# Four RMS norms and a last one: squares summed in column strips, roots spread by picked rows, two units that end one after the other

## The chip, the cores and the metric

The kernel runs on one core of a Trainium2 chip. The metric is device time in microseconds (us), and lower is better. TensorE (PE) multiplies and writes to PSUM; VectorE (DVE) and ScalarE (ACT) do the work by element; GpSimd (POOL) here only splits weights; SyncE (SP) issues most DMAs. The engines run their own instruction streams in order and wait for one another through semaphores.

## What is computed

One inference step of a small decoder of two layers, for a prompt of 1024 tokens and for 8 requests of 8 tokens. Layer 0 mixes with a gated linear recurrence, layer 1 with forgetting attention; each is followed by a gated feed-forward part (FFN) with a short convolution. The change concerns only the norms ahead of the projections:

```python
def _rmsnorm(x, g):
    n = x32 * lax.rsqrt(jnp.mean(x32 * x32, axis=-1, keepdims=True) + EPS)
    return n * g
def _modnorm(x, g, shift, scale):
    return _rmsnorm(x, g) * (1.0 + scale[:, None, :]) + shift[:, None, :]
...
    hn = _modnorm(x, norm_mix_g[l], sh1, sc1)      # before the mixer
    hn = _modnorm(x, norm_ffn_g[l], sh2, sc2)      # before the FFN
    hk = _modnorm(x, kv_norm_g, kv_shift, kv_scale)  # before K, V and forget logits
y = _rmsnorm(x, final_norm_g)
```

## The kernel before

**Layout.** The residual stream X holds channels on partitions: 8 tiles (k = 0 to 7) of 128 channels, each with T = 1090 columns (1026 for the prompt with its padding, 64 for the samples). A norm sums over channels, so over partitions and over the 8 tiles. A projection multiplies in three passes at the precision of fp32: the normed tile is kept as a high part HH and a low part HL, a unit of weights (8 k-tiles of 128 x 128) as WH and WL, and PE forms WH·HH, WL·HH and WH·HL, each in three pieces of 342, 342 and 406 columns.

**Norms.** There are six uses: norm 0 (recurrence), 1 (FFN of layer 0), 2 (K and V), 3 (queries; same X as norm 2, so its roots are reused), 4 (FFN of layer 1) and the final one, which goes straight to the output. ACT squares each tile into SQ (L1037), DVE adds seven of them into ACC (L1384). PE sums over partitions (L673 for ACC, L677 for the last SQ): the data are the weights, in nine blocks of 128 columns, and a column of ones streams, so that the sums land as 128 x 9. DVE and ACT form the reciprocal root on S9 (L1394, L1042, L1397 to L1400: mean, square root, reciprocal, one Newton step). DVE multiplies the identity by the nine columns (DIAG, L1402), PE spreads them over all partitions (L685), ACT copies them into RS (L1046).

**First use.** DVE scales a tile into TN (`scaled`, L1410), ACT adds the shift and rounds it into HH (`high`, L1053), DVE takes the rest as HL (`lowered`, L1427). The 64 sample columns of all 8 tiles go together (L1415 to L1419 on DVE, L1056 on ACT, L1426 on DVE), between tiles 0 and 1, and ACT signals the first HH tile only after them. PE takes the tiles as they come in `two_units` (L652): for each k both units u = 0 and 1, the three passes in turn, so that the two units end together.

**Order around it.** After `two_units` each later unit of the stage is one `unit_job` (L627). Its weights must be split by POOL (WH at L564, WL at L567), and POOL may overwrite a slot of WH and WL only when ACT has seen that the unit before in this slot is done (`got`, L1028). DMAs keep the raw weights ahead. ACT must also have emptied the slot in PSUM (`free`).

## Time and profile before

| | us |
|---|---|
| device time, median of 3 runs | 3282.46 (3279.54 to 3283.14) |
| profiled execution, device time | 3284.32 |
| its span, first to last instruction | 3282.9 |
| PE busy | 3060.2 (93% of the span) |
| POOL, DVE, ACT busy | 1121.4, 1372.9, 879.4 |
| granted PE clock, mean | 0.967 of full speed |

The profiled execution is 1.86 us above the median, and 1.4 us of it lie outside the span. In the rows below a timeline gives the start, the length, the engine, line and operation of each merged group, the number of records, and in brackets how long the engine had been idle and what ended that. A matmul of plain fp32 data leaves two records. The clock is a share of 2.4 GHz.

### The profile page before, as it was taken

The numbers are of one execution on the slowest core, as the hardware profiler recorded it, in microseconds if no ns is written. First come the engines' busy times: TensorE is split into PE (matmuls) and PEld (weight loads), VectorE is DVE, ScalarE is ACT, GpSimd is POOL, SyncE is SP. The second block draws the span as 40 slices with busy tenths as digits, with TensorE's granted clock in tenths as the row PEclk, the third lists the DMA queues.
The fourth block names the chain that finished last, engine by engine and source line by source line (L and its number), as shares of the span: only waits on it lengthen the run. The fifth ranks groups of instructions, "written<-read, shape, count | busy, mean of one in ns | idle before, by whom it ended". The sixth has DMA issues, their size and how long they took to land.

```text
span 3282.9 us, 49150 instructions
## 1 busy us (share of the span) xinstructions
PE 3060.2 (93%) x19242; PEld 2877.5 (88%) x19242; DVE 1372.9 (42%) x2024; ACT 879.4 (27%) x1453; POOL 1121.4 (34%) x571
## 2 busy tenths in 40 slices
PE   6999979899999999997997988888899999999996
PEld 4878859799999999997997866657899999999996
DVE  5345382443434444345103165542443434344344
ACT  3143170241312112122212145541141213121121
POOL 1312305333333333332332255524333333333331
PEclk9999989899999999998998989999899999999997
DMA  6644612111111111110543554664111111111111
GB/s 220 215 150 151 226 68 79 38 51 42 41 45 45 45 44 39 45 45 28 168 144 142 151 128 106 175 268 166 38 39 45 45 45 41 42 45 45 45 44 61
DMA packets 99465, 295.58 MB, mean 90 GB/s; under 512 B 14001, under 2 KB 15409, under 8 KB 99105
## 3 DMA queue, kind: packets, MB, share of 16 engines
q1 hardware_dynamic: 85616, 244.52, 22.5%
q10 hardware_dynamic: 13744, 49.61, 4.4%
q8 instruction: 73, 1.20, 0.1%
q14 instruction: 32, 0.25, 0.0%
HBM read 253.98 MB, written 40.10 MB: 90 GB/s over the span
## 4 chain that ended last, share of the span: by engine, by line
PE 65%; issue 11%; DVE 4%; POOL 3%; ACT 2%; DMA 1%; ACTq 0%; SPq 0%; POOLq 0%; DVEq 0%
PE PS L627 56%; PE PS L895 2%; POOL WH L564 2%; PE PS L878 2%; POOL WL L567 1%; PE PS L862 1%; PE PS L863 1%; ACT PX L1282 1%; PE PS L652 1%; DMA KB<-in_cache_k 0%; DMA X<-in_xT 0%; PE PS L909 0%; ACT PT L1272 0%; DVE X L1863 0%; PE PS L941 0%
## 5 line engine op out<-in xcount | busy, mean ns | idle before, releaser
L564 POOL TENSOR_TENSOR WH<-WRAW,ZERO 128x1024 fp32r<-128x1024 f32 x214 | 410.7, 1919 | 1868.9 <-ACTq L1028 1289.9
L627 PE MATMUL PS<-HH,WH 128*128 128x342 f32 (+1 forms) x3144 | 702.0, 332 | 28.1 <-POOL WL L567 24.9
L627 PE MATMUL PS<-HL,WH 128*128 128x342 f32 (+1 forms) x3144 | 701.9, 332 | 0.0
L627 PE MATMUL PS<-HH,WL 128*128 128x342 f32 (+1 forms) x3144 | 699.4, 331 | 0.0
L627 PEld LDWEIGHTS PS<-HH,WH 128*128 128x128 f32 x3144 | 559.3, 190 | 36.6 <-issue 18.8
L627 PEld LDWEIGHTS PS<-HH,WL 128*128 128x128 f32 x3144 | 562.3, 190 | 1.7
L627 PEld LDWEIGHTS PS<-HL,WH 128*128 128x128 f32 x3144 | 563.1, 190 | 0.2
L567 POOL TENSOR_TENSOR WL<-WRAW,WH 128x1024 fp32r<-128x1024 f32 x214 | 544.8, 2546 | 16.8
L1638 DVE SCALAR_TENSOR_TENSOR FC<-FU,FCW,FC 128x1026 f32<-128x1026 f32 x96 | 239.7, 2497 | 587.6 <-ACT FC L1140 587.6
L627 PE MATMUL PS<-AH,WH 128*128 128x342 f32 (+1 forms) x1152 | 256.9, 331 | 6.4 <-DVE AL L1656 4.9
L627 PE MATMUL PS<-AH,WL 128*128 128x342 f32 (+1 forms) x1152 | 255.4, 330 | 0.0
L627 PE MATMUL PS<-AL,WH 128*128 128x342 f32 (+1 forms) x1152 | 255.0, 330 | 0.0
L1135 ACT ACTIVATE FU<-PS 128x1026 f32<-128x1026 f32 x96 | 98.9, 1030 | 566.8 <-PE PS L627 566.8
L1448 DVE TENSOR_TENSOR XS<-PS,MOD 128x64 f32<-128x64 f32 x112 | 25.1, 224 | 499.2 <-PE PS L627 496.3
L1144 ACT ACTIVATE AH<-FC 128x1090 f32 (+1 forms) x48 | 53.7, 1120 | 660.2 <-DVE FC L1654 660.2
L627 PEld LDWEIGHTS PS<-AH,WH 128*128 128x128 f32 x1152 | 205.0, 190 | 8.5 <-DVE AL L1656 5.6
L627 PEld LDWEIGHTS PS<-AH,WL 128*128 128x128 f32 x1152 | 205.3, 189 | 0.9
L627 PEld LDWEIGHTS PS<-AL,WH 128*128 128x128 f32 x1152 | 205.2, 189 | 0.3
L1450 DVE SCALAR_TENSOR_TENSOR X<-PS,MOD,X 128x1026 f32 (+1 forms) x112 | 143.9, 1284 | 0.0
L1646 DVE SCALAR_TENSOR_TENSOR FC<-FU,FCW,FC 128x1026 f32<-128x1026 f32 x96 | 127.7, 1330 | 0.0
L1037 ACT ACTIVATE SQ<-X 128x1090 f32 x40 | 44.5, 1116 | 300.1 <-DVE X L1453 288.1
L1139 ACT ACTIVATE FC<-PS,FCW 128x1026 f32<-128x1026 f32 x96 | 116.5, 1214 | 0.0
(273 smaller groups left out, 3575.3 us busy)
## 6 DMA issues: line engine op xcount, KB each, us to landing
WRAW<-in_wstream SPq DMA_DIRECT2D x214, 512.0 KB, 3.5
MS<-in_mod_w SPq DMA_DIRECT2D x96, 512.0 KB, 6.8
KB<-in_cache_k SPq DMA_DIRECT2D x32, 512.0 KB, 8.8
VB<-in_cache_v SPq DMA_DIRECT2D x32, 512.0 KB, 8.0
K<-k_split SPq DMA_DIRECT2D x48, 256.0 KB
Q<-q_split SPq DMA_DIRECT2D x48, 256.0 KB
out_kv<-STG ACTq DMA_DIRECT2D x16, 545.0 KB, 3.2
MU<-in_mod_w SPq DMA_DIRECT2D x16, 512.0 KB, 12.5
```

The costliest lines, as they stand in the source:

```text
L564: pool.tensor_tensor(WH[:, u, :], WRAW[:, u, :], ZERO[:].broadcast_to([P, UNIT]), ALU.add).then_inc(hi.sem, 1)
L567: pool.tensor_tensor(WL[:, u, :], WRAW[:, u, :], WH[:, u, :].bitcast(F32), ALU.subtract).then_inc(S["split_done"], 1)
L627: mm = pe.matmul(PS[:, o:o + hi - lo], lhs(n), rhs[:, k, lo:hi], start=first and n == 0 and m == 0, stop=last and n == len(kts) - 1 and m ...
L878: mm = pe.transpose(PS[:, o + n * P:o + (n + 1) * P], tile[:, w_ + kt * P:w_ + (kt + 1) * P], ID[:])
L895: mm = pe.matmul(PS[rows, o + c:o + end], VS[p % 2][:, kt, rows], PT[:, e, st % RING, c:end], start=(i == 0 and c == lo), stop=True, skip_ ...
L1037: act.activation(SQ[:, u, :], X[:, i * 2 + u, :], ACT.Square).then_inc(S["act_sq"], 1)
L1135: act.activation(three(FU[:, s, 2:2 + S0]), prompt(s), ACT.Copy)
L1139: act.activation(three(FC[:, s, 0:S0]), prompt(s), ACT.Identity, **par)
L1144: act.activation(AH[:, c, :], FC[:, 0, :], ACT.Copy).then_inc(S["f_hi"], 1)
L1450: STT(three(X[:, k, 0:S0]), prompt(s), MOD[:, gate + k, 0:1], three(X[:, k, 0:S0]), ALU.mult, ALU.add).then_inc(free[s], 1)
L1638: STT(FC[:, s, 0:S0], FU[:, s, 1:1 + S0], FCW[:, idx, 1:2], FC[:, s, 0:S0], ALU.mult, ALU.add)\
L1646: STT(FC[:, s, 0:S0], FU[:, s, 0:S0], FCW[:, idx, 0:1], FC[:, s, 0:S0], ALU.mult, ALU.add)
```

## The change

Five things are changed. **Sums:** the ones become the weights, 32 columns of them, and the squares stream in four pieces of 273 columns, each into its own strip of 32 partitions; the sums land on 128 partitions x 273 columns, 32 rows alike in each strip. **Roots:** the steps on DVE and ACT work on 128 x 273 (SV). A square root of a single element (WARM) stands ahead of the wait for the mean. DIAG is gone: PE multiplies SV by a column of the identity repeated 128 times, which picks row 32j, so that quarter j appears on all partitions. **First tile:** ACT copies, DVE scales and ACT rounds tile 0 quarter by quarter, and PE starts unit 0 on the first two column pieces. **Samples:** they come after tile 1. **Two units:** the lows of tiles 0 and 1 come after the highs of both, and tiles 5, 6, 7 are done for unit 0 first, then for unit 1. Norm 3 has only the last two. The core of the diff (memory and semaphore names left out):

```diff
@@ -100,17 +100,19 @@
     return done // KT - 1 if done // KT > (done - bursts(unit)) // KT else None
-SPREAD = ((0, 3), (3, 6), (6, 9))
-def position(j):
-    return min(P * j, T - P)
+QUARTER = 273
+ROOT_AT = (0, 1536, 2048, 2560)
+def quarter(j):
+    return min(QUARTER * j, T - QUARTER)
 U_RG, U_OUT, U_FFN, U_LF, U_D = 2 * RT, 2 * KT, 2 * FT + NG * GC, 2, KT
 UNITS_1 = U_RG + U_OUT + U_FFN + U_LF + 3 * U_D
 UNITS_2 = U_D + U_FFN
+SHARED = 5
 PIECES = ((0, PC), (PC, 2 * PC), (2 * PC, T))
...
@@ -635,24 +638,50 @@
             pe.wait_ge(free[u].sem, free[u].next())
             job(u, tiles(WH, u), tiles(WL, u), xh, xl, range(KT), fresh=fresh).then_inc(ready[u], 1)
-        def two_units():
+        def two_units(roots_in_psum=True):
+            def part_of(k, u, pieces, lows):
+                for m, (w_, x) in enumerate(((WH, HL),) if lows else ((WH, HH), (WL, HH))):
+                    for c in pieces:
+                        lo, hi = PIECES[c]
+                        o = SLOT[u] + 512 * c
+                        mm = pe.matmul(PS[:, o:o + hi - lo], w_[:, u, k * P:(k + 1) * P], x[:, k, lo:hi],
+                                       start=k == 0 and m == 0 and not lows, stop=k == KT - 1 and lows)
+                return mm
             for u in range(2):
                 pe.wait_ge(split.sem, split.next())
+            if roots_in_psum:
+                for c in range(2):
+                    pe.wait_ge(part.sem, part.next())
+                    part_of(0, 0, (c,), False)
+            for u in range(2):
                 pe.wait_ge(free[u].sem, free[u].next())
-            for k in range(KT):
-                for m, (w_, x) in enumerate(((WH, HH), (WL, HH), (WH, HL))):
-                    if m == 0:
-                        pe.wait_ge(hh.sem, hh.next())
-                    if m == 2:
-                        pe.wait_ge(hn.sem, hn.next())
-                    for u in range(2):
-                        for c, (lo, hi) in enumerate(PIECES):
-                            o = SLOT[u] + 512 * c
-                            mm = pe.matmul(PS[:, o:o + hi - lo], w_[:, u, k * P:(k + 1) * P], x[:, k, lo:hi],
-                                           start=k == 0 and m == 0, stop=k == KT - 1 and m == 2)
-                        if k == KT - 1 and m == 2:
-                            mm.then_inc(ready[u], 1)
+            pe.wait_ge(hh.sem, hh.next())
+            for u in range(roots_in_psum, 2):
+                part_of(0, u, (0, 1), False)
+            pe.wait_ge(hh.sem, hh.next())
+            for u in range(2):
+                part_of(1, u, (0, 1), False)
+            pe.wait_ge(his.sem, his.next())
+            for k in range(2):
+                for u in range(2):
+                    part_of(k, u, (2,), False)
+            for k in range(2):
+                pe.wait_ge(hn.sem, hn.next())
+                for u in range(2):
+                    part_of(k, u, (0, 1, 2), True)
+            for k, units in [(k, (0, 1)) for k in range(2, SHARED)] + [(k, (u,)) for u in range(2) for k in range(SHARED, KT)]:
+                if units[0] == 0:
+                    pe.wait_ge(hh.sem, hh.next())
+                for u in units:
+                    part_of(k, u, (0, 1, 2), False)
+                if units[0] == 0:
+                    pe.wait_ge(hn.sem, hn.next())
+                for u in units:
+                    mm = part_of(k, u, (0, 1, 2), True)
+                    if k == KT - 1:
+                        mm.then_inc(ready[u], 1)
         def proj(xh, xl, pairs, fresh=None):
...
@@ -669,23 +698,18 @@
             pe.wait_ge(acc.sem, acc.next(KT - 1))
             acc.next()
             pe.wait_ge(free[0].sem, free[0].next())
-            for j in range(9):
-                pe.matmul(PS[:, 1524 + j:1525 + j], ACC[:, position(j):position(j) + P], ONES[:, 0:1],
-                          start=j == 0, stop=True, skip_group_check=True)
+            for j in range(4):
+                pe.matmul(PS[32 * j:32 * j + 32, 0:QUARTER], ONES[:, 0:32], ACC[:, quarter(j):quarter(j) + QUARTER],
+                          start=True, stop=True, skip_group_check=True)
             pe.wait_ge(sq.sem, sq.next(KT))
-            for j in range(9):
-                mm = pe.matmul(PS[:, 1524 + j:1525 + j], SQ[:, 1, position(j):position(j) + P], ONES[:, 0:1],
+            for j in range(4):
+                mm = pe.matmul(PS[32 * j:32 * j + 32, 0:QUARTER], ONES[:, 0:32], SQ[:, 1, quarter(j):quarter(j) + QUARTER],
                                start=False, stop=True, skip_group_check=True)
             mm.then_inc(ready[0], 1)
-            for c, (a, b) in enumerate(SPREAD):
-                pe.wait_ge(diag.sem, diag.next())
-                for lo, hi in ((a, min(b, 8)), (8, b)):
-                    if hi > lo:
-                        n = min(P * hi, T) - P * lo
-                        mm = pe.matmul(PS[:, 512 * c + P * (lo - a):512 * c + P * (lo - a) + n], ONES[:],
-                                       DIAG[:].rearrange("p j x -> p (j x)")[:, P * hi - n:P * hi], start=lo == a, stop=True,
-                                       skip_group_check=True)
-                mm.then_inc(S["rs_psum"], 1)
+            pe.wait_ge(rows_done.sem, rows_done.next())
+            for j, o in enumerate(ROOT_AT):
+                pe.matmul(PS[:, o:o + QUARTER], ID[:, 32 * j:32 * j + 1].broadcast_to([P, P]), SV[:, 2, :],
+                          start=True, stop=True).then_inc(S["rs_psum"], 1)
         def mod_product(x, buf, sem, landed):
...
@@ -1038,23 +1062,37 @@
         def roots():
             ready[0].next()
+            act.activation(WARM[:], ZERO[:], ACT.Sqrt)
             act.wait_ge(var.sem, var.next())
-            act.activation(S9[:, 1, :], S9[:, 0, :], ACT.Sqrt).then_inc(S["rs_root"], 1)
-            for c, (a, b) in enumerate(SPREAD):
-                act.wait_ge(spread.sem, spread.next())
-                n = min(P * b, T) - P * a
-                ins = act.activation(RS[:, P * a:P * a + n], PS[:, 512 * c:512 * c + n], ACT.Copy)
+            act.activation(SV[:, 1, :], SV[:, 0, :], ACT.Sqrt).then_inc(S["rs_root"], 1)
+        def kept(j):
+            act.wait_ge(spread.sem, spread.next())
+            a, b = QUARTER * j, min(QUARTER * j + QUARTER, T)
+            o = ROOT_AT[j] + a - quarter(j)
+            ins = act.activation(RS[:, a:b], PS[:, o:o + b - a], ACT.Copy)
             ins.then_inc(S["act_root"], 1)
         def high(n):
             for k in range(KT):
-                act.wait_ge(tn.sem, tn.next())
                 sh = NORMS[n][0] + k
-                ins = act.activation(HH[:, k, 0:S0], TN[:, k % 2, 0:S0], ACT.Identity, bias=MOD[:, sh, 0:1])
-                if k == 0:
+                if k == 0 and n != 3:
+                    kept(0)
+                    for j in range(4):
+                        if j < 3:
+                            kept(j + 1)
+                        act.wait_ge(tn.sem, tn.next())
+                        a, b = QUARTER * j, min(QUARTER * j + QUARTER, S0)
+                        ins = act.activation(HH[:, 0, a:b], TN[:, 0, a:b], ACT.Identity, bias=MOD[:, sh, 0:1])
+                        if j in (1, 2):
+                            ins.then_inc(S["hi_part"], 1)
+                else:
+                    act.wait_ge(tn.sem, tn.next())
+                    ins = act.activation(HH[:, k, 0:S0], TN[:, k % 2, 0:S0], ACT.Identity, bias=MOD[:, sh, 0:1])
+                ins.then_inc(S["act_hi"], 1)
+                if k == 1:
                     act.wait_ge(S["dve_tns"], n + 1)
-                    ins = act.activation(HH[:, :, S0:T], TNS[:], ACT.Copy)
-                ins.then_inc(S["act_hi"], 1)
+                    act.activation(HH[:, :, S0:T], TNS[:], ACT.Copy).then_inc(S["act_his"], 1)
         def norm(n, sums=True):
             if sums:
...
@@ -1390,18 +1430,22 @@
             sq.next()
             dve.sem_inc(accs.sem, 1)
             accs.next()
-            v, r, y, z = (S9[:, n, :] for n in range(4))
-            TSC(v, PS[:, 1524:1533], 1.0 / D, EPS, ALU.mult, ALU.add).then_inc(S["dve_var"], 1)
+            v, r, y, z = (SV[:, n, :] for n in range(4))
+            TSC(v, PS[:, 0:QUARTER], 1.0 / D, EPS, ALU.mult, ALU.add).then_inc(S["dve_var"], 1)
             dve.wait_ge(var.sem, var.next())
             dve.wait_ge(roots.sem, roots.next())
             chain(dve.reciprocal(y, r))
             chain(STT(z, y, -0.5, y, ALU.mult, ALU.mult))
             chain(TT(z, z, v, ALU.mult))
-            chain(STT(y, z, 1.5, y, ALU.add, ALU.mult))
-            for a, b in SPREAD:
-                TT(DIAG[:, a:b, :], ID[:].unsqueeze(1).broadcast_to([P, b - a, P]),
-                   y[:, a:b].unsqueeze(2).broadcast_to([P, b - a, P]), ALU.mult).then_inc(S["rs_diag"], 1)
-            dve.wait_ge(root.sem, root.next())
+            STT(y, z, 1.5, y, ALU.add, ALU.mult).then_inc(S["rs_rows"], 1)
+        def first_scaled(n):
+            for j in range(4):
+                a, b = QUARTER * j, min(QUARTER * j + QUARTER, S0)
+                dve.wait_ge(root.sem, root.next())
+                STT(TN[:, 0, a:b], X[:, 0, a:b], MOD[:, NORMS[n][1], 0:1], RS[:, a:b], ALU.mult, ALU.mult)\
+                    .then_inc(S["dve_tn"], 1)
             dve.sem_inc(free[0], 1)
         def scaled(n, k):
...
@@ -1422,18 +1466,22 @@
             dve.wait_ge(hi.sem, hi.next())
             sh = NORMS[n][0] + k
+            ins = STT(HL[:, k, 0:S0], TN[:, k % 2, 0:S0], MOD[:, sh, 0:1], HH[:, k, 0:S0].bitcast(F32), ALU.add, ALU.subtract)
             if k == 0:
-                TT(HL[:, :, S0:T], TNS[:], HH[:, :, S0:T].bitcast(F32), ALU.subtract)
-            STT(HL[:, k, 0:S0], TN[:, k % 2, 0:S0], MOD[:, sh, 0:1], HH[:, k, 0:S0].bitcast(F32), ALU.add, ALU.subtract)\
-                .then_inc(los.sem, 1)
+                dve.wait_ge(S["act_his"], n + 1)
+                ins = TT(HL[:, :, S0:T], TNS[:], HH[:, :, S0:T].bitcast(F32), ALU.subtract)
+            ins.then_inc(los.sem, 1)
             los.next()
         def norm(n, sums=True):
             if sums:
                 rms()
-            scaled(n, 0)
+            if n != 3:
+                first_scaled(n)
+            else:
+                scaled(n, 0)
+            scaled(n, 1)
             scaled_samples(n)
-            scaled(n, 1)
             for k in range(KT):
                 lowered(n, k)
                 if k + 2 < KT:
...
@@ -1859,6 +1907,8 @@
         dve.wait_ge(xdone.sem, xdone.next(KT))
         ffn(1)
         rms()
+        dve.wait_ge(root.sem, root.next(4))
+        dve.sem_inc(free[0], 1)
         for k in range(KT):
             STT(X[:, k, :], X[:, k, :], NGAIN[:, 5, k:k + 1], RS[:], ALU.mult, ALU.mult).then_inc(S["dve_tn"], 1)
```

On PE, from the sums of norm 1 into its two units (PS is PSUM, ID the identity; the operand that streams is named first). Before:

```order
L673 MATMUL PS<-ONES,ACC 128x1 x9
L677 MATMUL PS<-ONES,SQ 128x1 x9
L685 MATMUL PS<-DIAG,ONES 128x384 x2
L685 MATMUL PS<-DIAG,ONES 128x256
L685 MATMUL PS<-DIAG,ONES 128x66
L652 MATMUL PS<-HH,WH 128x342 x2
L652 MATMUL PS<-HH,WH 128x406
L652 MATMUL PS<-HH,WH 128x342 x2
L652 MATMUL PS<-HH,WH 128x406
```

After:

```order
L702 MATMUL PS<-ACC,ONES 32x273 x4
L706 MATMUL PS<-SQ,ONES 32x273 x4
L711 MATMUL PS<-SV,ID 128x273 x4
L648 MATMUL PS<-HH,WH 128x342
L648 MATMUL PS<-HH,WL 128x342
L648 MATMUL PS<-HH,WH 128x342
L648 MATMUL PS<-HH,WL 128x342
L648 MATMUL PS<-HH,WH 128x342 x2
L648 MATMUL PS<-HH,WL 128x342 x2
L648 MATMUL PS<-HH,WH 128x342 x2
```

Eighteen sums with data as weights became eight with ones as weights, and the first two pieces of tile 0 of unit 0 stand alone ahead of the rest.

On PE, the end of the same two units and the first job of the next pair. Before:

```order
L652 MATMUL PS<-HH,WL 128x342 x2
L652 MATMUL PS<-HH,WL 128x406
L652 MATMUL PS<-HH,WL 128x342 x2
L652 MATMUL PS<-HH,WL 128x406
L652 MATMUL PS<-HL,WH 128x342 x2
L652 MATMUL PS<-HL,WH 128x406
L652 MATMUL PS<-HL,WH 128x342 x2
L652 MATMUL PS<-HL,WH 128x406
L135 UNCONDITIONAL_BRANCH
L135 ISA
L635 REGISTER_ALU
L627 MATMUL PS<-HH,WH 128x342 x2
```

After:

```order
L648 MATMUL PS<-HL,WH 128x342 x2
L648 MATMUL PS<-HL,WH 128x406
L648 MATMUL PS<-HH,WH 128x342 x2
L648 MATMUL PS<-HH,WH 128x406
L648 MATMUL PS<-HH,WL 128x342 x2
L648 MATMUL PS<-HH,WL 128x406
L648 MATMUL PS<-HL,WH 128x342 x2
L648 MATMUL PS<-HL,WH 128x406
L137 UNCONDITIONAL_BRANCH
L137 ISA
L638 REGISTER_ALU
L630 MATMUL PS<-HH,WH 128x342 x2
```

Before, unit 0 ends two rows ahead of unit 1 (the last four HL rows are 0, 0, 1, 1); after, these rows are all of unit 1, and unit 0 has ended eighteen rows ahead of the end.

On ACT, norm 2, behind the store of the FFN's state. Before:

```order
L1164 DMA out_fst<-FST 128x864
L1042 ACT_TABLE_LOAD [waits dve_var]
L1042 ACTIVATE S_92<-S_92 128x9 [waits ffn_out]
L1046 ACTIVATE RS<-PS 128x384 [waits rs_psum] x2
L1046 ACTIVATE RS<-PS 128x322 [waits rs_psum]
L1053 ACTIVATE HH<-TN,MOD 128x1026 [waits dve_tn]
```

After:

```order
L1202 DMA out_fst<-FST 128x864
L1065 ACT_TABLE_LOAD
L1065 ACTIVATE WARM<-ZERO 128x1 [waits ffn_out]
L1067 ACTIVATE SV<-SV 128x273 [waits dve_var]
L1073 ACTIVATE RS<-PS 128x273 [waits rs_psum] x2
L1086 ACTIVATE HH<-TN,MOD 128x273 [waits dve_tn]
L1073 ACTIVATE RS<-PS 128x273 [waits rs_psum]
L1086 ACTIVATE HH<-TN,MOD 128x273 [waits dve_tn]
L1073 ACTIVATE RS<-PS 128x271 [waits rs_psum]
```

The load of the table for the square root carried the wait for the mean; now it carries none, and the copies of the roots alternate with the quarters of tile 0.

## Rows read from the trace of the kernel before

**Rows 1.** The page, part 4: the chain that ended last, by engine.

```profile
PE 65%; issue 11%; DVE 4%; POOL 3%; ACT 2%; DMA 1%; ACTq 0%; SPq 0%; POOLq 0%; DVEq 0%
```

**Rows 2.** Timeline of norm 1: start, length, engine, line, operation, records, [idle before].

```profile
606.73 4.00 PE L673 MATMUL PS<-ONES,ACC 128*128 128x1 f32 x18 [3.44 <-DVE ACC L1384]
...
614.71 0.17 DVE L1394 TENSOR_SCALAR S<-PS 128x9 f32<-128x9 f32 x1 [8.03 <-DVEq L1391]
...
615.23 0.21 DVE L1397 RECIPROCAL S<-S 128x9 f32<-128x9 f32 x1 [0.35 <-ACT S L1042]
...
616.71 4.11 PE L685 MATMUL PS<-DIAG,ONES 128*128 128x384 f32 x8 [2.13 <-DVE DIAG L1402]
...
618.39 0.49 ACT L1046 ACTIVATE RS<-PS 128x384 f32<-128x384 f32 x1 [3.26 <-PE PS L685]
...
621.45 1.29 DVE L1410 SCALAR_TENSOR_TENSOR TN<-X,MOD,RS 128x1026 f32<-128x1026 f32 x1 [3.86 <-ACT RS L1046]
...
625.60 2.15 PE L652 MATMUL PS<-HH,WH 128*128 128x342 f32 x6 [4.79 <-ACT HH L1056]
...
650.50 1.16 PE L652 MATMUL PS<-HL,WH 128*128 128x342 f32 x6
```

**Rows 3.** Timeline, from the end of the two units of norm 1 on.

```profile
651.29 1.89 POOL L564 TENSOR_TENSOR WH<-WRAW,ZERO 128x1024 fp32r<-128x1024 f32 x1 [42.40 <-ACTq L1028]
...
655.74 0.76 PE L627 MATMUL PS<-HH,WH 128*128 128x342 f32 x3 [4.08 <-POOL WL L567]
```

**Rows 4.** Stretches: us, busy PE, PEld, DVE, ACT, POOL (records), PE clock, DMA.

```profile
625.60:629.40 3.80, 3.80 (x13) 3.77 (x14) 3.76 (x5) 1.40 (x2) 0.00 (x0) 0.50 0.02 4
629.40:651.60 22.20, 22.20 (x133) 21.93 (x131) 14.68 (x13) 7.01 (x7) 0.31 (x1) 1.00 0.00 1
...
655.74:660.38 4.64, 4.64 (x19) 4.60 (x19) 4.64 (x5) 3.27 (x6) 4.56 (x2) 0.63 0.35 115
```

**Rows 5.** Timeline of norm 0, eight records of four strips at 32 columns.

```profile
22.11 1.08 PE L699 MATMUL PS<-MU,CTP 128*32 128x256 f32 x8 [0.18 <-DMA MU<-in_mod_w]
```

**Rows 6.** Groups by line on DVE: count | busy us, mean ns | idle before.

```profile
L1761 DVE RECIPROCAL RIN<-SUMS 128x1 f32<-128x1 f32 x128 | 17.8, 156 | 20.1 <-ACT PY L1282 18.9 <-ACT PX L1282 0.3
...
L1415 DVE TENSOR_TENSOR TNS<-X,RS 128x512 f32<-128x512 f32 x5 | 3.4, 685 | 0.0
...
L1397 DVE RECIPROCAL S<-S 128x9 f32<-128x9 f32 x5 | 1.1, 214 | 4.4 <-ACT S L1042 4.4
```

**Rows 7.** Timeline of norm 0 and of the recurrence behind it.

```profile
31.25 4.00 PE L673 MATMUL PS<-ONES,ACC 128*128 128x1 f32 x18
...
35.89 1.89 POOL L564 TENSOR_TENSOR WH<-WRAW,ZERO 128x1024 fp32r<-128x1024 f32 x1
...
37.86 2.34 POOL L567 TENSOR_TENSOR WL<-WRAW,WH 128x1024 fp32r<-128x1024 f32 x1
...
50.98 1.29 DVE L1410 SCALAR_TENSOR_TENSOR TN<-X,MOD,RS 128x1026 f32<-128x1026 f32 x1
...
85.38 1.28 PE L627 MATMUL PS<-HH,WH 128*128 128x342 f32 x3 [4.00 <-POOL WL L567]
...
87.70 2.37 POOL L567 TENSOR_TENSOR WL<-WRAW,WH 128x1024 fp32r<-128x1024 f32 x1
87.71 3.44 DVE L1555 SCALAR_TENSOR_TENSOR XC<-RU,RGP,XC 128x1026 f32<-128x1026 f32 x1
```

**Rows 8.** Timeline of norm 2 on ACT, and of PE behind norm 3.

```profile
1518.07 1.28 ACT L1042 ACT_TABLE_LOAD   x1 [8.05 <-DVE S L1394]
...
1798.98 1.27 PE L627 MATMUL PS<-HH,WH 128*128 128x342 f32 x3 [4.08 <-POOL WL L567]
```

**Rows 9.** Timeline of the final norm.

```profile
3251.74 4.00 PE L673 MATMUL PS<-ONES,ACC 128*128 128x1 f32 x18 [4.70 <-DVE ACC L1384]
...
3267.81 10.21 DVE L1863 SCALAR_TENSOR_TENSOR X<-X,NGAIN,RS 128x1090 f32<-128x1090 f32 x8 [3.87 <-ACT RS L1046]
```

**Rows 10.** Timeline of PE late in the FFN of layer 0.

```profile
1464.10 0.77 PE L627 MATMUL PS<-AH,WH 128*128 128x342 f32 x3 [2.47 <-DVE AL L1656]
```

More of the change, by code:

```diff
@@ L195, in trunk @@
     ZERO = c("ZERO", [P, 1])
+    WARM = c("WARM", [P, 1])
     TINY = c("TINY", [P, 1])
@@ L221, in trunk @@
     n_.off = O_R3 + 2 * TB
-    DIAG = n_("DIAG", [P, 9, P])
-    S9 = n_("S9", [P, 4, 9])
+    SV = n_("SV", [P, 4, QUARTER])
     assert n_.off <= O_R3 + 16384
@@ L347, in trunk @@
         mu0 mu1 mu2 mu3 mu4 mu5 mu6 mu7 ms0 ms1 ms2 ms3 ms4 ms5 mods_used consts filled sigmoid silu mods_row mods_turned mods_tile mods_done lam_exp sp_done x_in
-        act_sq dve_acc dve_var rs_root rs_diag rs_psum act_root act_hi dve_tn dve_tns dve_lo act_self dve_self
+        act_sq dve_acc dve_var rs_root rs_rows rs_psum act_root hi_part act_his act_hi dve_tn dve_tns dve_lo act_self dve_self
         rg_halo gate_w0 gate_w1 conv_free xc_ready act_tanh act_sqrt pair_free
@@ L612, in _ @@
         acc, hn, hh = Count(S["dve_acc"], 2), Count(S["dve_lo"], 1), Count(S["act_hi"])
-        sq, diag = Count(S["act_sq"]), Count(S["rs_diag"])
+        sq, rows_done = Count(S["act_sq"]), Count(S["rs_rows"])
+        part, his = Count(S["hi_part"]), Count(S["act_his"])
         act_chunk = Count(S["act_ready"], 1)
@@ L846, in _ @@
         turn_values(1)
-        two_units()
+        two_units(roots_in_psum=False)
         proj(HH, HL, KT // 2 - 1)
@@ L1357, in _ @@
         roots()
+        for j in range(4):
+            kept(j)
         for k in range(KT):
@@ L1399, in rms @@
             chain(TT(z, z, v, ALU.mult))
-            chain(STT(y, z, 1.5, y, ALU.add, ALU.mult))
-            for a, b in SPREAD:
-                TT(DIAG[:, a:b, :], ID[:].unsqueeze(1).broadcast_to([P, b - a, P]),
-                   y[:, a:b].unsqueeze(2).broadcast_to([P, b - a, P]), ALU.mult).then_inc(S["rs_diag"], 1)
-            dve.wait_ge(root.sem, root.next())
+            STT(y, z, 1.5, y, ALU.add, ALU.mult).then_inc(S["rs_rows"], 1)
+        def first_scaled(n):
+            for j in range(4):
+                a, b = QUARTER * j, min(QUARTER * j + QUARTER, S0)
+                dve.wait_ge(root.sem, root.next())
+                STT(TN[:, 0, a:b], X[:, 0, a:b], MOD[:, NORMS[n][1], 0:1], RS[:, a:b], ALU.mult, ALU.mult)\
+                    .then_inc(S["dve_tn"], 1)
             dve.sem_inc(free[0], 1)
```

## The prediction, made before the changed kernel was run

> **What bounds the kernel now.** I read the chain that ended last first: 65% of it is PE, and 11% is time in which nothing was waited for [rows 1]; PE is busy 93% of the span. So a change pays only where PE stands still or runs at its low clock. Next I read the timeline around each norm. The reader is to see three stretches in norm 1 [rows 2]. The sums occupy PE from 606.73 until DVE reads them at 614.71, 7.98 us. From there the roots go DVE, ACT, DVE, PE, ACT, DVE in single file, and PE's first product comes at 625.60. The two units then end at 650.50 + 1.16 = 651.66. The third stretch is the handover: unit 0 ends with unit 1, POOL begins to split the next weights only then, and PE waits 4.08 us [rows 3]. Last I read the clock: at the restarts the granted clock is 0.50, and 13 matmuls take 3.80 us, 0.30 each; at full clock 133 take 22.20, 0.167 each [rows 4]. After the handover 19 matmuls take 4.64 us instead of 19 x 0.167 = 3.17, so each handover costs 1.5 us more than its wait. It is 2.0 where the first three take 1.27 or 1.28 us and not 0.76 [rows 3, 7, 8].
>
> **Sums.** Eighteen sums (36 records) become eight (16 records). The nearest row has eight records in four strips of 32 columns, 256 columns long: 1.08 us together [rows 5]. Scaled to 273 columns that is 1.15, twice is 2.3, with 0.13 to reach DVE 2.4: 5.6 us less. Bounds: at full clock about half, 1.2; if strips ran one after another, a record would cost what it does in L685, where two records for each of 1090 columns fill 4.11 us [rows 2]: 273 x 4.11 / 2180 = 0.51, and sixteen 8.2. I take the strips, since rows 5 have their form.
>
> **Roots.** The instructions now have 273 columns instead of 9. A DVE instruction of 512 columns took 685 ns [rows 6], so 273 take about 0.44; the root on ACT I put at 0.41, near the 0.49 of a copy of 384 columns [rows 2]. The reciprocal is not seen at this width: 156 ns for one column, 214 for nine [rows 6], 7 ns a column, so 2.0 us. Bounds are 0.44, if that slope is start-up alone, and 2.4. With the mean, root, reciprocal, three Newton steps and six handovers: 0.44 + 0.41 + 2.0 + 3 x 0.48 + 0.2 = 4.5 us to PE's start, against 2.0 before (616.71 - 614.71) [rows 2].
>
> The Trainium skill (VectorE: DVE Perf Modes, "First, the fixed hardware budget") says that the reciprocal repeats a divide step 8 times in the pipe; at the 0.96 GHz given there I estimate 8.3 ns a column, 2.4 us. By that the time would be 1.6 us longer; rows 6 fit the same kind of slope, slightly smaller.
>
> Spread: four multiplications of 273 columns are 1092 instead of 1090, in the same form, so some 4.1 us on PE as before. DVE began 621.45 - 616.71 = 4.74 after PE [rows 2]; the last copy on ACT is a little shorter now, 4.6. The fourth quarter takes DVE 0.4. ACT's four copies and four roundings alternate, 0.8 a quarter, and stay within PE's 1.0.
>
> **First tiles.** Tile 0 is through DVE 2.4 + 4.5 + 4.6 + 0.4 = 11.9 after the sums begin, at 618.6. The early quarters are nearly free: they fill PE, but do not set the end. What is late next is DVE's row: tile 1, three sample instructions, low of tile 0, low of the samples, tile 2, low of tile 1. That is four of 1.29 and four of 0.685, 7.9 us, to 626.5; PE has done all highs of tiles 0 and 1 and the lows of tile 0 by then. It still needs the lows of tile 1 (1.0 us) and six tiles of 18 matmuls (6 x 3.01), and ends at 645.8, 5.9 us before 651.66. DVE needs two instructions of 1.29 a tile against PE's 3.0, so it stays ahead. The samples behind tile 1 and the lows behind the highs cost nothing as long as this cover holds; the bound without it is given under the low clock.
>
> **Handover.** Unit 0 now ends 27 matmuls, 4.5 us, before unit 1. POOL needs 655.74 - 651.29 = 4.45 us from unit 0's end to PE's next weights [rows 3]; ACT empties the slot meanwhile. So the wait of 4.1 and the slow restart of 1.5 go, but the margin is only 0.1. Five stretches have it: 4.00, 4.08 and 4.08 in the rows [rows 3, 7, 8], and two more like them behind norms 2 and 4.
>
> **Sum by norm.** Norms 1 and 4: 5.9 + 4.1 + 1.5 = 11.5 each. Norm 2: the same and the table load of 1.28, which stood behind the mean [rows 8] and now runs during the sums; 12.8. WARM waits there for ACT's store of the FFN's state, as the root did before, and the root is queued behind it; the store was over by the mean before, and the 2.4 us of the sums cover most of it now. Norm 3 has no sums; PE starts after the first HH tile, 621.45 + 1.29 + 1.3 against 625.60 in norm 1's rows, so 1.5 earlier; with 4.1 and 2.0: 7.6. Final norm: 16.07 us from sums to output before [rows 9]; now 2.4 + 4.5 + 4.6 = 11.5; 4.6 less.
>
> Norm 0 gains less at the front. POOL splits two units there until 40.20 [rows 7]. A DVE instruction with two operands in SBUF stands still while POOL works: 3.44 us instead of 1.29, ending 1.08 after POOL's 2.37 [rows 7]. The first Newton step would come at 31.25 + 2.4 + 3.0 = 36.6, waits for POOL's WH (37.78), and POOL's WL gets in ahead of the second, which ends near 40.8. The spread begins at 41.3; before, 31.25 + 9.98 = 41.2. So the 5.6 us of the sums are eaten here. Tile 0 begins near 51.0 as before, since the modulation products stand behind the spread; in quarters it takes 2.7, then 7.9 and the 19.3 from there to the end in norm 1: 80.9, against 50.98 + 30.2 = 81.2. With 0.3, 4.0 and 2.0: 6.3.
>
> 6.3 + 11.5 + 12.8 + 7.6 + 11.5 + 4.6 = 54.3 us. Against the profiled execution's own 3284.32 that is 3230.0; this execution lies 1.86 above the median, so 3228 (the final norm's table load is part of its 16.07).
>
> **Rivals.** *The handover stays.* POOL's split takes longer than the tail (it shares its way to SBUF with DVE, whose last lows come 0.6 us earlier): with 0.1 us of margin PE could wait again. Fully, 5 x 5.8 = 29 us return: 3257. Against it: POOL's and DVE's instructions stand there in the same order as before. 0.08.
>
> *The strips run one after another*, so that the change doesn't do what it says: 8.3 instead of 2.4, as much as before or more; over five sums 28 us return, 3256. Rows 5 speak against it. 0.04.
>
> *The reciprocal is cheap*: 1.55 us less in norms 1, 2, 4 and the last (in norm 0 POOL decides), 6 in all, 3222. The two widths in rows 6 speak against it. 0.13.
>
> *The clock stays low, slower than before.* PE's first work after the spread is now broken by waits for quarters, samples and lows. If the granted clock stayed at 0.50 through two units, 144 matmuls at 0.30 take 43.5 us from 617.8, where the first quarters are ready: the end is 661.3 instead of 645.8, 15.5 us, five times 77: 3305. It decides from 11 us of loss per norm, some 83 of 144 matmuls at the low level. Rows speak both ways: after a wait of 4.08 us the clock fell [rows 3, 4], after one of 2.47 three matmuls took the usual 0.77 [rows 10], and the new waits are near 1 us. 0.03.
>
> [...]
>
> **How the numbers follow.** The forecast, 3228, has 0.72. The range takes in the cheap reciprocal and a spread at full clock (four times 1.8 more), 3214; on the other side a slow stretch of 1.6 us in five norms, handovers of 0.5 us left and the 2.4 us reciprocal, 16 us, 3244. The handover in full, the serial strips and the low clock are left out, 0.15. A measurement can tell about 0.2% (6.6 us) from no change. Faster by more: 0.96; slower by more: 0.03 with its milder forms; within: 0.01.
>
> **What would show it.** Right: from the first sum to DVE's mean 2.4 us in all five; a reciprocal near 2.0; two units that end 39 us after the sums begin, with PE idle about 1 us ahead of the lows of tile 1; PE's next job without idle time and without a stretch at clock 0.50; Newton steps of 1.5 and 2.5 us in norm 0 only. Wrong: idle time on PE before L630 ended by POOL's WL, reciprocals near 0.4, sums near 7 us, or a clock of 0.50 in the two units. The forecast fails most easily by the reciprocal, which enters four times on the path, and by the margin of 0.1 us at the handover.

## The result

The changed kernel takes 3230.05 us (median of four executions, 3229.67 to 3235.14); the kernel before took 3281.49 beside it. The ratio is 0.9847, with a 95% interval of 0.983 to 0.9864. The prediction was 3228, between 3214 and 3244.

The spans of the two profiled executions, 3282.9 and 3228.3, differ by 54.6 us; the forecast's sum was 54.3. That the two agree so closely is partly luck, as the parts below show. By the medians the change is worth 51.4 us: the profiled execution of the kernel before lies 2.8 us above that kernel's median, the one after at its own.

### The profile page after: what moved, and what is told of

Its sections match the earlier page's. It is cut to its first block, busy times and chain, and to the rows that moved or that the text cites. A ratio compares the mean times of both kernels' runs of the same rounds, so it can differ in the third digit from the quotient of the medians.

```text
span 3228.3 us, 48968 instructions
## 1 busy us (share of the span) xinstructions
PE 3026.4 (94%) x19142; PEld 2833.4 (88%) x19142; DVE 1383.6 (43%) x2021; ACT 884.3 (27%) x1475; POOL 1121.9 (35%) x571
## 4 chain that ended last, share of the span: by engine, by line
PE 66%; issue 10%; DVE 4%; POOL 3%; ACT 2%; DMA 1%; ACTq 0%; SPq 0%; POOLq 0%; DVEq 0%
PE PS L630 57%; PE PS L919 2%; POOL WH L566 2%; PE PS L902 2%; POOL WL L569 1%; PE PS L886 1%; PE PS L887 1%; ACT PX L1320 1%; DMA KB<-in_cache_k 1%; DMA X<-in_xT 0%; PE PS L648 0%; ACT PT L1310 0%; PE PS L933 0%; DVE X L1913 0%; PE PS L965 0%
```

## The profile after

The chain that ended last has hardly moved: 66% of it is PE and 10% is time in which nothing was waited for, against 65% and 11% before [rows 1].

```profile
PE 66%; issue 10%; DVE 4%; POOL 3%; ACT 2%; DMA 1%; ACTq 0%; SPq 0%; POOLq 0%; DVEq 0%
```

So the gain is to be looked for in the norms. This is the timeline of norm 1 in the changed kernel (start, length, engine, line, operation, records, [idle before]); it answers to [rows 2, 3].

```profile
601.67 1.14 PE L702 MATMUL PS<-ACC,ONES 128*32 128x273 f32 x8 [3.44 <-DVE ACC L1424]
602.58 1.14 PE L706 MATMUL PS<-SQ,ONES 128*32 128x273 f32 x8
603.88 0.44 DVE L1434 TENSOR_SCALAR SV<-PS 128x273 f32<-128x273 f32 x1 [2.27 <-DVEq L1431]
604.36 0.43 ACT L1067 ACTIVATE SV<-SV 128x273 f32<-128x273 f32 x1 [2.51 <-DVE SV L1434]
604.90 1.86 DVE L1437 RECIPROCAL SV<-SV 128x273 f32<-128x273 f32 x1 [0.57 <-ACT SV L1067]
...
608.25 3.68 PE L711 MATMUL PS<-SV,ID 128*128 128x273 f32 x8 [4.54 <-DVE SV L1440]
...
612.34 0.39 PE L648 MATMUL PS<-HH,WH 128*128 128x342 f32 x1 [0.41 <-ACT HH L1086]
...
612.51 0.43 DVE L1447 SCALAR_TENSOR_TENSOR TN<-X,MOD,RS 128x207 f32<-128x207 f32 x1 [0.19 <-ACT RS L1073]
...
620.57 1.26 PE L648 MATMUL PS<-HL,WH 128*128 128x342 f32 x6 [0.91 <-DVE HL L1469]
...
635.58 1.90 POOL L566 TENSOR_TENSOR WH<-WRAW,ZERO 128x1024 fp32r<-128x1024 f32 x1 [31.75 <-ACTq L1052]
...
637.55 2.41 POOL L569 TENSOR_TENSOR WL<-WRAW,WH 128x1024 fp32r<-128x1024 f32 x1
...
639.29 0.66 PE L648 MATMUL PS<-HL,WH 128*128 128x342 f32 x3
...
640.09 0.76 PE L630 MATMUL PS<-HH,WH 128*128 128x342 f32 x3
```

The reader is to see three things. DVE reads the sums 2.21 us after they begin, where it was 7.98. The two units end at 639.29 + 0.66 = 639.95, 38.28 after the sums began, where it was 651.66 - 606.73 = 44.93. And PE goes on at 640.09: POOL now begins at 635.58, while unit 1 still runs, and is through at 639.96, level with PE.

The next view gives TensorE's granted clock in the 4.64 us from PE's first product of the next weights on, behind norms 0, 1, 2, 3 and 4 (stretch, length, busy PE with its records, clock, DMA share, GB/s). Behind norm 1, 19 matmuls ran at a mean clock of 0.63 there [rows 4]; now it is 28 at full clock, in all five places.

```profile
80.02:84.66 4.64, 4.64 (x28) 1.00 1.05 407
640.09:644.73 4.64, 4.64 (x28) 1.00 0.36 118
1532.48:1537.12 4.64, 4.64 (x28) 1.00 0.84 239
1764.17:1768.81 4.64, 4.64 (x28) 1.00 1.11 421
2347.56:2352.20 4.64, 4.64 (x28) 1.00 0.30 113
```

The table sets the time from the first sum to PE's first product of the next weights against the forecast. In norm 3, which has no sums, it counts from the first product of the two units, and that came 30.22 us earlier than before where POOL's last split ahead of it came 28.83 earlier: 1.4 more. "Restart" is the matmuls missing from 28 in the view just shown, before, times 0.167 us (records before: 15, 19, 18, 15 and 19).

| norm | before | after | shorter | restart | together | forecast |
|---|---|---|---|---|---|---|
| 0 | 54.13 | 48.84 | 5.3 | 2.2 | 7.5 | 6.3 |
| 1 | 49.01 | 38.42 | 10.6 | 1.5 | 12.1 | 11.5 |
| 2 | 50.25 | 38.60 | 11.65 | 1.7 | 13.3 | 12.8 |
| 3 | 30.32 | 25.73 | 4.6 + 1.4 | 2.2 | 8.2 | 7.6 |
| 4 | 48.90 | 37.71 | 11.2 | 1.5 | 12.7 | 11.5 |
| final, to its output | 16.07 | 11.19 | 4.9 | | 4.9 | 4.6 |

Together that is 58.7 us, 4.4 more than forecast. The span shows 54.6, so 4.1 us were given back between the norms. The largest piece lies at the output projection of the recurrence. The first two rows are DVE and PE there in the changed kernel, the next two the same places before; then the first 5 us of that unit on PE, after and before (busy PE, PEld, DVE, ACT, POOL, then clock).

```profile
490.32 0.97 DVE L1655 MEMSET ACC<- 128x1090 f32 x1 [6.49 <-DMA X<-in_xT]
495.89 1.27 PE L630 MATMUL PS<-YH,WH 128*128 128x342 f32 x3 [2.38 <-POOL WL L569]
```

```profile
496.60 0.97 DVE L1607 MEMSET ACC<- 128x1090 f32 x1 [5.27 <-DMA X<-in_xT]
502.20 0.77 PE L627 MATMUL PS<-YH,WH 128*128 128x342 f32 x3 [1.19 <-POOL WL L567]
```

```profile
495.89:500.89 5.00, 5.00 (x22) 4.98 (x23) 0.00 (x0) 0.00 (x0) 4.18 (x2) 0.71 0.31 105
```

```profile
502.20:507.20 5.00, 5.00 (x30) 5.00 (x31) 0.00 (x0) 0.00 (x0) 4.19 (x2) 1.00 0.35 108
```

The state X comes back by one transfer of 4.36 MB, which landed 15.9 us after its issue here and 14.7 before (after first, then before):

```profile
X<-in_xT ACTq DMA_DIRECT2D x1, 4360.0 KB, 15.9
```

```profile
X<-in_xT ACTq DMA_DIRECT2D x1, 4360.0 KB, 14.7
```

DVE waits for it, POOL for DVE and PE for POOL: PE lost 1.19 us more to the wait and 8 matmuls of 0.167 us, 1.3, to a slow restart that the kernel before didn't have. That is 2.5 of the 4.1. The transfer was issued 7.5 us earlier than before, at 474.06 instead of 481.56, and took 1.2 longer. It took 15.6 to 15.9 us in every kernel here that has the new norms and loads X in one transfer, even where it was issued at 480.62 (the handover undone, below), and 14.7 in the two with the old norms. So the longer transfer comes with the new norms, and not with the earlier issue; why is open. A second piece is pure clock. Late in the FFN of layer 0 PE waits 2.47 us for DVE in both kernels [rows 10]; in the 5 us behind it, before ran 27 matmuls at full clock and after 21 at 0.66 (the wait in the changed kernel, then the stretch behind it before and after):

```profile
1446.93 0.76 PE L630 MATMUL PS<-AH,WH 128*128 128x342 f32 x3 [2.47 <-DVE AL L1704]
```

```profile
1464.10:1469.10 5.00, 4.80 (x27) 1.00 0.00 0
```

```profile
1446.93:1451.93 5.00, 5.00 (x21) 0.66 0.00 0
```

Six matmuls of 0.167 are 1.0 us. The remaining 0.6 is spread over small shifts that were not traced further.

## Experiments

All stand beside runs of the kernel before on the same chip, which gave 3281.28 to 3282.2 in the three sets. "After" is the changed kernel, 3230.05. It was not run again beside them, so where the times differ by less than 3 us the traces carry the reading. The strips of the sums, and the order of the samples and of the lows, were not tried by themselves.

**The handover, undone.** After, with the last tiles in turn again:

```diff
-SHARED = 5
+SHARED = KT
```

> The changed kernel, but the last three tiles are streamed to both units in turn again, as the first five are, so that unit 0 ends with unit 1. Theory (the handover): POOL's split of the next weights begins 4.5 us later against PE, so idle time of 4.0 to 4.1 us ended by POOL's WL stands ahead of L630 again in five places, each with a slow restart worth 1.5 to 2.0 us: 29 us more than the changed kernel's 3230, so 3256 to 3262. Rival (the new order of the tiles does the work, and the handover would be hidden by the earlier end of the sums): no wait at those places, 3229 to 3233.

Measured: 3262.64, 32.6 more, as the first theory said and a little beyond its range. The timeline behind norm 1 shows the old wait; the rows under it are the clock view at norms 1 and 4.

```profile
650.72 1.27 PE L630 MATMUL PS<-HH,WH 128*128 128x342 f32 x3 [4.08 <-POOL WL L569]
```

```profile
650.72:655.36 4.64, 4.64 (x15) 0.50 0.36 118
...
2378.94:2383.58 4.64, 4.64 (x19) 0.63 0.32 113
```

The wait is that of before to the hundredth. The restart is dearer: in four of five places 15 matmuls run in 4.64 us, in the kernel before in two of five. Against the kernel before, norm 1 runs four matmuls fewer in that time and norm 2 three; seven times 0.167 us is 1.2 of the 3.6 us by which the middle of the forecast, 3259, was short. Another 2.1 lies in the units of norms 3 and 4: they end 26.80 us after their first product and 38.44 after the sums begin, in the changed kernel 25.59 and 37.58.

**The handover alone.** The kernel before, with the tail taken unit by unit:

```diff
+SHARED = 5
...
-            for k in range(KT):
+            for k, units in [(k, (0, 1)) for k in range(SHARED)] + [(k, (u,)) for u in range(2) for k in range(SHARED, KT)]:
                 for m, (w_, x) in enumerate(((WH, HH), (WL, HH), (WH, HL))):
...
-                    for u in range(2):
+                    for u in units:
```

> The kernel before, with one part of the change alone: the last three tiles of the two units are streamed unit by unit. Theory (the parts add up): the five handover waits and slow restarts go, 29 us less than 3282: 3250 to 3256, and the sums, roots and first tiles stay where they were. Rival (the parts cover each other: with the old sums PE reaches the tail at the low clock or DVE's lows come late there): less than 15 us, above 3267.

Measured: 3256.45, half a us above the theory's range and far from the rival's. No idle time stands at the five handovers (in norm 0, PE goes on 49.21 us after the sums begin, against 54.13 before). So in norm 0 the tail alone brings what the whole change brings there (48.84), as the prediction had it, which gave everything else 0.3 us in that norm. By spans the two halves are 3260.7 - 3228.3 = 32.4 and 3255.0 - 3228.3 = 26.7, 59.1 against 54.6 for the whole: the handover is worth 4.5 us more beside the new norms than beside the old. 1.2 of it is the dearer restart just named. Another 0.6 lies between the first sums (in norm 3, the first product) and PE's next job, summed over the five places: the handover shortens these stretches by 22.0 us beside the new norms and by 21.4 beside the old. The remaining 2.7 lies between the norms and stays open.

**POOL beside the Newton steps.** After, with POOL's second split at the start behind the first roots:

```diff
         split(0, None)
+        pool.wait_ge(S["rs_rows"], 1)
         split(1, None)
```

> The changed kernel, but at the start POOL begins the second unit's split only when DVE has the first roots' rows ready. Theory (in norm 0 the Newton steps stand still because POOL works beside them): the steps of 1.85 and 2.46 us become 0.45 each, the spread begins at 37.8 instead of 41.2, the modulation products behind it move as much, and the time falls by 3.4 us to 3226 to 3228. Rival 1 (the products are bound by their weights' DMA): the steps become short, the time stays at 3229 to 3231. Rival 2 (the long steps have nothing to do with POOL): steps of 1.85 and 2.46 as before.

Measured: 3228.37 (3222.79 to 3230.26), 0.4 above the theory's range. Norm 0 in the changed kernel first, then in this one:

```profile
34.42 1.86 DVE L1437 RECIPROCAL SV<-SV 128x273 f32<-128x273 f32 x1 [0.56 <-ACT SV L1067]
...
36.32 1.85 DVE L1438 SCALAR_TENSOR_TENSOR SV<-SV 128x273 f32<-128x273 f32 x1
37.95 2.42 POOL L569 TENSOR_TENSOR WL<-WRAW,WH 128x1024 fp32r<-128x1024 f32 x1
...
38.21 2.46 DVE L1439 TENSOR_TENSOR SV<-SV 128x273 f32<-128x273 f32 x1
...
41.20 3.90 PE L711 MATMUL PS<-SV,ID 128*128 128x273 f32 x8 [7.98 <-DVE SV L1440]
```

```profile
36.10 0.45 DVE L1439 SCALAR_TENSOR_TENSOR SV<-SV 128x273 f32<-128x273 f32 x1
...
36.58 0.44 DVE L1440 TENSOR_TENSOR SV<-SV 128x273 f32<-128x273 f32 x1
...
37.56 4.01 PE L712 MATMUL PS<-SV,ID 128*128 128x273 f32 x8 [4.56 <-DVE SV L1441]
```

The steps of 1.85 and 2.46 us become 0.45 and 0.44, the spread begins 3.6 us earlier, and PE's next job comes 45.99 after the first sum instead of 48.84. The profiled execution is 2.9 us shorter. The median, 1.7 us lower, scatters too much to say so by itself; the trace does. The reciprocal, which has one operand, took 1.86 beside POOL as it did without.

**The first tile whole.** After, with tile 0 in one piece (the parts of ACT and PE are left out):

```diff
-            for j in range(4):
-                a, b = QUARTER * j, min(QUARTER * j + QUARTER, S0)
-                dve.wait_ge(root.sem, root.next())
-                STT(TN[:, 0, a:b], X[:, 0, a:b], MOD[:, NORMS[n][1], 0:1], RS[:, a:b], ALU.mult, ALU.mult)\
...
+            dve.wait_ge(root.sem, root.next(4))
+            STT(TN[:, 0, 0:S0], X[:, 0, 0:S0], MOD[:, NORMS[n][1], 0:1], RS[:, 0:S0], ALU.mult, ALU.mult)\
```

> The changed kernel, but the first tile is scaled, raised to its high part and streamed in one piece, after all four copies of the roots. Theory (DVE's row after tile 0 sets the end, the early quarters only fill PE): DVE is through tile 0 0.85 us later (1.29 instead of 0.43 after the last copy), the two units of norms 0, 1, 2 and 4 end 0.85 us later, 3.4 in all: 3232 to 3235. Rival (the early start of PE is what the quarters bring): PE begins 2.7 us later in four norms and ends as much later, 10.8 in all: 3239 to 3243.

Measured: 3231.38, 1.3 more than after and just below the theory's range. The rows of norm 1:

```profile
612.43 1.29 DVE L1436 SCALAR_TENSOR_TENSOR TN<-X,MOD,RS 128x1026 f32<-128x1026 f32 x1 [4.28 <-ACT RS L1069]
...
615.05 0.91 PE L648 MATMUL PS<-HH,WH 128*128 128x342 f32 x2 [3.09 <-ACT HH L1079]
...
620.01 1.28 DVE L1458 SCALAR_TENSOR_TENSOR HL<-TN,MOD,HH 128x1026 fp32r<-128x1026 f32 x1
...
620.65 2.16 PE L648 MATMUL PS<-HL,WH 128*128 128x342 f32 x12
```

PE begins the units 13.43 after the sums and not 10.67, 2.76 later, and yet ends them at 39.22 and not 38.28, 0.94 later; in norm 2 it is 3.0 and 0.95, in norm 4 3.0 and 1.98, and norm 0 ends 0.42 earlier. So the rival, an end as late as the start, is refuted. But the theory's 0.85 is met in norms 1 and 2 without its mechanism: here PE never waits for DVE. The low of tile 1 is ready at 621.29, and PE, which streams the lows of tiles 0 and 1 in one run of twelve, needs it at 621.66. PE's own late start, at the low clock, sets the end here, while in the changed kernel DVE's row does (PE waits 0.91 for it at 620.57). In norm 4 the clock is low for longer behind the start (0.66 over the first 8.2 us, 0.80 and 0.79 in norms 1 and 2), and the end is 1.98 later. The 3.5 us of the four norms show as 1.0 in the span, since stretches between norms ran a little faster here (from the sums of norm 2 to those of norm 4, 815.13 against 815.97).

**The reciprocal.** After, with the inverse root on ACT (the zero's root ahead of the wait is replaced likewise, with ones as its input):

```diff
-            act.activation(SV[:, 1, :], SV[:, 0, :], ACT.Sqrt).then_inc(S["rs_root"], 1)
+            act.activation(SV[:, 2, :], SV[:, 0, :], ACT.Abs_reciprocal_sqrt).then_inc(S["rs_root"], 1)
...
-            chain(dve.reciprocal(y, r))
```

> The changed kernel, but ACT forms the inverse root itself, in the one instruction that formed the root, and DVE's reciprocal of 273 columns is gone; the Newton steps stay. Theory (the reciprocal of 1.86 us stands on the path of every norm but the first): from mean to spread 2.5 us instead of 4.37 in norms 1, 2, 4 and the last, 7.6 us in all, and 0 to 2.2 in norm 0, where POOL still holds the Newton steps: 3220 to 3223. Rival 1 (something else is late next, such as the tile's modulation or DVE's row): under 3 us, 3227 or more. Rival 2 (the function's table must be loaded on the path): 1.28 us are lost again in three or four norms: 3225 to 3228.

Measured: 3220.26, 9.8 less, within the theory's range. Norm 1:

```profile
604.49 0.43 ACT L1067 ACTIVATE SV<-SV 128x273 f32<-128x273 f32 x1 [1.13 <-DVE SV L1434]
605.03 0.44 DVE L1437 SCALAR_TENSOR_TENSOR SV<-SV 128x273 f32<-128x273 f32 x1 [0.58 <-ACT SV L1067]
...
606.48 4.01 PE L711 MATMUL PS<-SV,ID 128*128 128x273 f32 x8 [2.64 <-DVE SV L1439]
```

From mean to spread it is 606.48 - 604.01 = 2.47 us, where it was 4.37. The two units of norm 1 end 36.60 after the sums, 1.7 earlier than 38.28; the table load that norm 1 now needs lies beside the sums. In norm 0 the first products come 0.2 us earlier only: the Newton steps move into POOL's time and take 1.89, 2.02 and 2.46. The Trainium skill (ScalarE: Activation LUTs, "What it computes") advises a root on ScalarE with VectorE's reciprocal, because of the accuracy of the inverse root there; it does not speak of this function, and the Newton step behind it was kept here.

**The length of the tail.** After, with two tiles unit by unit, and with four:

```diff
-SHARED = 5
+SHARED = 6
```

> The changed kernel, but only the last two tiles, not three, are streamed unit by unit: unit 0 ends 18 matmuls, 3.0 us, ahead of unit 1, and POOL needs 4.5. Theory: PE waits 1.5 us at the five handovers. If the clock holds over such a wait, 7.5 us more: 3236 to 3239. Rival (the clock falls at any wait there, and the slow restart of 1.5 to 2.4 comes with it): 3245 to 3250.

```diff
-SHARED = 5
+SHARED = 4
```

> The changed kernel, but the last four tiles, not three, are streamed unit by unit: unit 0 ends 36 matmuls, 6.0 us, ahead of unit 1. Theory (POOL needs 4.5 us, and 27 matmuls cover it): nothing is left to gain, at most 0.14 us at each of five places, 3229 to 3231. Rival (the handover is still short by what POOL loses beside DVE): 2 to 5 us less, 3225 to 3228.

Measured: 3237.61 with two and 3233.61 with four. With two tiles, the handovers of norms 0 and 1 read:

```profile
82.00 0.77 PE L630 MATMUL PS<-HH,WH 128*128 128x342 f32 x3 [1.52 <-POOL WL L569]
...
644.27 0.76 PE L630 MATMUL PS<-HH,WH 128*128 128x342 f32 x3 [1.59 <-POOL WL L569]
```

All five waits are 1.5 to 1.6 us, the first three matmuls behind them take the usual 0.76, and the time is 7.6 us more, where the five waits are 7.9: the wait alone, no restart. (The four executions lie far apart, from 3232.11 to 3240.94.) With four tiles both theories were wrong. The handover is free, and a new wait stands in unit 0's tail:

```profile
633.19 0.77 PE L648 MATMUL PS<-HL,WH 128*128 128x342 f32 x3 [0.31 <-DVE HL L1469]
...
635.71 0.77 PE L648 MATMUL PS<-HL,WH 128*128 128x342 f32 x3 [0.75 <-DVE HL L1469]
```

The two waits recur in norms 0, 2 and 4, and make 4.2 us in all. One unit alone uses up a tile in 9 matmuls, 1.5 us, and DVE makes one in two instructions of 1.28, 2.5 us. The shared tiles, at 3.0 us each, give DVE its lead; four tiles of the tail eat it. Three is long enough for POOL and short enough for DVE.

**The zero's root.** After, without the root of one zero ahead of the wait for the mean:

```diff
-            act.activation(WARM[:], ZERO[:], ACT.Sqrt)
```

> The changed kernel without the root of one zero that goes ahead of the wait for the mean. Theory (the table load then stands behind the mean wherever ACT reaches the root after the mean's wait is open for it, as before in norm 2 and the last): 1.28 us on the path in those two, 2.6 in all: 3232 to 3233, and from mean to spread 5.7 us instead of 4.37 there. Rival (the load is issued ahead of the wait in any case): 3229 to 3231.

Measured: 3232.62, 2.6 more, the theory's number. From mean to spread it is 5.70 us in norm 2 and 5.71 in the last, as forecast. ACT in norm 2:

```profile
1497.34 1.28 ACT L1066 ACT_TABLE_LOAD   x1 [2.69 <-DVE SV L1433]
1498.64 0.43 ACT L1066 ACTIVATE SV<-SV 128x273 f32<-128x273 f32 x1
```

What reaches the end is less: the units of norm 2 end 1.36 us later, and the output of the last norm begins 12.11 us after its sums and not 11.19, 0.92 later. That is 2.3; the rest lies elsewhere, and that the number fits so well is partly luck.

**The returning state.** After, with the transfer in two:

```diff
-        act.dma_start(X[:], I["xT"].rearrange("k p t -> p k t")).then_inc(S["x_back"], 16)
+        for n, (a, b) in enumerate(((0, 2), (2, KT))):
+            act.dma_start(X[:, a:b], I["xT"].rearrange("k p t -> p k t")[:, a:b]).then_inc(S[f"x_back{n}"], 16)
...
+            if rest:
+                dve.wait_ge(S[rest], 16)
```

> The changed kernel, but the state that comes back ahead of the recurrence's output projection is loaded in two transfers, tiles 0 and 1 first. Theory (part of norm 0's gain is given back there: DVE waits for the whole transfer of 4.36 MB, POOL for DVE, and PE for POOL, 2.4 us and a slow restart): PE doesn't wait for POOL at the third unit of that projection, and 3 to 4 us go: 3226 to 3227. Rival (the wait is only moved to the later tiles, or PE waits for something else there): 3229 to 3231.

Measured: 3225.72, 4.3 less and 0.3 below the theory's range. From PE's next job behind norm 0 to the sums of norm 1 it is 518.07 us here and 521.65 in the changed kernel: 3.6 less, as the theory has it. The other differences lie elsewhere (norm 0 itself took 1.0 longer here). DVE goes on 0.40 us after its own last instruction, and PE has no wait for POOL in that projection; the next idle time of PE behind its second unit is one of 0.23:

```profile
485.10 0.97 DVE L1656 MEMSET ACC<- 128x1090 f32 x1 [0.40 <-DVE YL L1644]
```

```profile
510.01 0.76 PE L630 MATMUL PS<-YH,WH 128*128 128x342 f32 x3 [0.23 <-issue]
```

**All three.** After, with the inverse root on ACT, POOL's late second split and the transfer in two:

> The changed kernel with three edits at once: ACT's inverse root in place of the reciprocal, POOL's second split at the start behind the first roots' rows, and the returning state in two transfers. Theory (each on the path, each in its own place): 7.6 and 2.9 and 3.5 us, and with POOL out of the way the 1.9 of the reciprocal in norm 0 too: 16 us less, 3212 to 3217. Rival (they cover each other, or the output projection gives it back): above 3221.

Measured: 3213.68 (3212.79 to 3216.78), within the theory's range. Its ratio to the kernel before is 0.9789 (0.9773 to 0.9805), outside the interval of the changed kernel: it is the fastest of all that ran. The gains add up: 16.4 us below the changed kernel, against 9.8, 1.7 and 4.3 by the medians one by one. One term of the theory did not come, though: the 1.9 us of the reciprocal in norm 0. With the reciprocal gone, the first Newton step stands beside POOL's split of the first unit and takes as long:

```profile
34.76 1.89 DVE L1439 SCALAR_TENSOR_TENSOR SV<-SV 128x273 f32<-128x273 f32 x1 [0.57 <-ACT SV L1068]
...
37.65 4.01 PE L712 MATMUL PS<-SV,ID 128*128 128x273 f32 x8 [4.09 <-DVE SV L1441]
```

The spread begins 6.14 us after the sums, and 6.24 where POOL alone is late.

## Why the prediction was right, and where it was not

**Sums.** 2.4 us forecast, 2.2 measured in norms 0, 1, 2 and the last, 1.30 in norm 4, where the sixteen records ran at full clock (1.00 granted; 0.50 in norm 1). The rival of strips in single file is refuted by the rows: eight records take 1.14 us.

**Roots.** 4.5 forecast, 608.25 - 603.88 = 4.37 measured. The reciprocal took 1.86 against a forecast of 2.0, 6.3 ns a column beyond the first ((1864 - 156) / 272), and the rival of a cheap one falls. The estimate of 2.4 from the Trainium skill (VectorE: DVE Perf Modes, "First, the fixed hardware budget") was too long by 0.5 us; a cost per column, as it has it, is there. That the reciprocal stands on the path is shown by the kernel without it.

**Norm 0.** Newton steps of 1.5 and 2.5 were forecast and are 1.85 and 2.46; the spread was to begin at 41.3 and began at 41.20. The cause, POOL, is shown by delaying it.

**First tiles.** Tile 0 was to be through 11.9 us after the sums begin and was at 612.94 - 601.67 = 11.27; DVE's row was to take 7.9 and took 7.6; the units were to end at 39.1 and ended at 38.28. The first two terms are 0.6 and 0.3 too long; from the row's end to the end of the units it took 19.4 for 19.3. Together they make 0.8 us a norm. That DVE's row decides is shown by PE's wait of 0.91 for it; the whole tile shows that the early quarters bring 0.9 us in norms 1 and 2 and not the 2.8 by which PE starts earlier.

**Handover.** The forecast said that the margin is only 0.1 us: PE goes on 0.04 to 0.14 after its last matmul. The restart was sized at 1.5 or 2.0 and is 1.5 to 2.2 by the matmuls counted; in the kernel with the handover put back it is 2.2 in four places.

**The clock.** The rival of a low clock through the two units did not come: behind a spread at 0.60, the first 8.2 us of the units in norm 1 ran at 1.00, through waits of 0.41, 0.92 and 0.91. In norms 2 and 4 it was 0.93 and 0.88. Only norm 0 began low, 0.63 over its first 8.2 us, and its units still ended 1.3 us sooner after the sums than before. Waits of 1.5 us at the handover did not bring the low clock about either.

**The step that failed** is that the sum let every us gained in a norm last to the end. It named what is late next inside each norm, but not behind it. The norms gave 58.7 where 54.3 were forecast, and 4.1 of it went at places that the change doesn't touch: at a transfer whose landing set DVE's start and which took 1.2 us longer, and at a wait after which the clock fell in one execution and not in the other. The total came out right because an excess and a loss of nearly one size met. A second, small step did not hold either: 1.86 us were taken off since the profiled execution of before lay above its median; that of after, with 3229.8, lies at its own. And the upper end of the range was summed wrongly: the terms named for it, 8.0, 2.5 and 1.6, make 12.1 us and not 16, so 3240 and not 3244; the measured time lies below either.

## What to carry to other kernels

Where two outputs share a streamed operand, let them part before the end, by as many products as the next operand's preparation takes; then look at what feeds the faster lone stream, since a longer tail outruns it. When work is squeezed ahead of a large transfer or a two-input vector instruction beside GpSimd, look behind the gain for who sets the next start: here 2.5 us were given back at a load that only two of its eight tiles made urgent. Count a reciprocal by its columns before widening a chain of small instructions.

## What the runs showed of the chip beyond expectation

The clock behind a wait is not set by the wait's length alone. After the same 4.08 us, 15 matmuls ran in 4.64 us in some places and 19 in others; after the same 2.47, 27 matmuls ran in 5 us in one kernel and 21 in the other; after the same 3.37 ahead of norm 4's sums, DVE had the mean 1.30 us later in the changed kernel and 2.22 in the one with the handover put back. Behind the five waits of 1.5 to 1.6 the clock didn't fall. What decides stays open.

ACT's inverse root of 273 columns takes 0.43 us, as its root does; DVE's reciprocal takes 1.86 for the same columns, beside a working POOL or without one.
